# A weight's low half two steps behind its high half, and a fresh order at four borders

## The reference, cut to what matters

```python
def swiglu(x, w_gate, w_up, w_down):                 # D_MODEL = 1024, D_FF = 2816
    return (jax.nn.silu(x @ w_gate) * (x @ w_up)) @ w_down

# block 1:  x + 0.5 * swiglu(rms_norm(x)), mixer, x + 0.5 * swiglu(rms_norm(x))
# block 2, per layer l, for the sequence h and (not after the last mixer) the context hc:
mod = jax.nn.silu(c) @ w_ada[l] + b_ada[l]           # nine vectors: shift, scale, gate, three times
h = h + HALF * gt1 * swiglu_2(ada_norm(h, g_ffn1[l], sh1, sc1), w1_ffn1[l], w3_ffn1[l], w2_ffn1[l])
# then a mixer of three branches, then a second feed-forward network, and at the end a norm
```

## Time and profile before

| what | value |
|---|---|
| time, median of 3 runs | 2787.03 us (2784.63 to 2797.26) |
| time of the profiled execution | 2783.03 us |
| its span, first to last instruction | 2781.2 us |
| PE busy | 2639.6 us, 95% of the span |
| DVE busy | 1713.1 us, 62% |
| ACT busy | 1060.0 us, 38% |
| TensorE's granted clock, mean | 0.970 |
| from HBM | 377.40 MB, 136 GB/s over the span |

### The profile page before, as it was taken

The page is one execution under the profiler, slowest core; times in us unless marked ns, Lnnn a source line. Parts: engine busy times, 40 slices in busy tenths (PEclk is TensorE's granted clock), DMA queues, the critical chain, the costliest instruction groups (busy, mean ns, idle before and its releaser), DMA issues.

```text
span 2781.2 us, 38461 instructions
## 1 busy us (share of the span) xinstructions
PE 2639.6 (95%) x15690; PEld 2305.1 (83%) x15690; DVE 1713.1 (62%) x2717; ACT 1060.0 (38%) x1594; POOL 142.0 (5%) x112
## 2 busy tenths in 40 slices
PE   7999878899999999998999999999999999989998
PEld 7997778899888888766878888888888887689898
DVE  6767464677767656655645567756545446766664
ACT  5445432445422223333243422323322224454553
POOL 0001023000000000032010000000000000310000
PEclk9999889899999999999999999999999999999999
DMA  7774200477455543211323255543444433135564
GB/s 246 231 231 163 71 22 1 132 247 229 143 182 172 183 152 113 58 38 46 99 86 104 84 192 179 170 157 121 138 141 130 134 106 112 57 122 179 168 190 151
DMA packets 110113, 380.97 MB, mean 137 GB/s; under 512 B 12017, under 2 KB 17393, under 8 KB 109553
## 3 DMA queue, kind: packets, MB, share of 16 engines
q1 hardware_dynamic: 108928, 373.32, 42.1%
q10 hardware_dynamic: 1008, 5.18, 0.5%
HBM read 377.40 MB, written 1.05 MB: 136 GB/s over the span
## 4 chain that ended last, share of the span: by engine, by line
PE 86%; DVE 7%; ACT 4%; issue 2%; POOL 1%; DMA 1%; SPq 0%; ACTq 0%; DVEq 0%
PE B L1363 25%; PE B L1365 24%; PE B L1364 24%; PE B L1585 2%; DVE w_lo L1914 2%; ACT w_hi L1654 1%; POOL TMP L2338 1%; PE B L1601 1%; PE B L1378 1%; PE B L1509 1%; PE B L1379 1%; PE B L1380 1%; PE B L1495 1%; PE B L1502 1%; DVE AC L2175 1%
## 5 line engine op out<-in xcount | busy, mean ns | idle before, releaser
L1363 PE MATMUL B<-U,w_hi 128*128 128x256 f32 (+1 forms) x2896 | 959.9, 331 | 9.4 <-DVE w_lo L1914 5.6
L1364 PE MATMUL B<-U,w_hi 128*128 128x256 f32 (+1 forms) x2896 | 953.4, 329 | 0.0
L1365 PE MATMUL B<-U,w_lo 128*128 128x256 f32 (+1 forms) x2896 | 953.0, 329 | 0.0
L1914 DVE TENSOR_TENSOR w_lo<-w_raw,w_hi 128x1024 fp32r<-128x1024 f32 (+4 forms) x587 | 685.2, 1178 | 414.0 <-ACT w_hi L1654 413.3
L1654 ACT ACTIVATE w_hi<-w_raw 128x1024 fp32r<-128x1024 f32 (+4 forms) x587 | 591.0, 1012 | 519.0 <-PE B L1365 487.1
L1363 PEld LDWEIGHTS B<-U,w_hi 128*128 128x128 f32 x2896 | 549.0, 190 | 67.7 <-issue 13.2
L1364 PEld LDWEIGHTS B<-U,w_hi 128*128 128x128 f32 x2896 | 549.2, 190 | 52.5 <-issue 1.3
L1365 PEld LDWEIGHTS B<-U,w_lo 128*128 128x128 f32 x2896 | 548.6, 189 | 51.7
L1363 PE MATMUL B<-HHf,w_hi 128*128 128x256 f32 (+1 forms) x1122 | 363.9, 324 | 5.8 <-DVE w_lo L1914 5.8
L1364 PE MATMUL B<-HLf,w_hi 128*128 128x256 f32 (+1 forms) x1122 | 362.8, 323 | 0.0
L1365 PE MATMUL B<-HHf,w_lo 128*128 128x256 f32 (+1 forms) x1122 | 362.8, 323 | 0.0
(11 more groups left out here) (337 smaller groups left out, 2675.5 us busy)
## 6 DMA issues: line engine op xcount, KB each, us to landing
w_raw<-in_w SPq DMA_DIRECT2D x504, 512.0 KB, 4.3
w_ada<-in_w SPq DMA_DIRECT2D x144, 512.0 KB, 3.5
w_raw<-in_w SPq DMA_DIRECT2D x58, 384.0 KB, 3.5
w_raw<-in_w SPq DMA_DIRECT2D x16, 240.0 KB, 2.6
X<-in_x SPq DMA_DIRECT2D x2, 1024.0 KB, 9.6
w_raw<-in_w SPq DMA_DIRECT2D x8, 256.0 KB, 3.1
BW<-in_bias ACTq DMA_DIRECT2D x1, 1536.0 KB, 10.4
K<-in_consts ACTq DMA_DIRECT2D x2, 640.0 KB, 4.5
```

Source lines behind the costliest of these rows:

```text
L1363: pe.matmul(o, hi, xh, start=i == 0 and s.start, stop=False)
L1364: pe.matmul(o, hi, xl, start=False, stop=False)
L1365: e = pe.matmul(o, lo, xh, start=False, stop=i == last and s.stop)
L1914: dve.tensor_tensor(w_lo[:, plan.slot[u], 0:n], w_raw[:, plan.ring[u], 0:n], w_hi[:, plan.slot[u], 0:n].bitcast(F32), ALU.subtract).then_i ...
```

## The change

It has five parts. The split of a unit becomes two steps: `split_hi` stands where `split` stood, and `split_lo` follows when LATER = 2 more steps have been put down, or at once if the next step uses the unit. SP's refill of `w_raw` goes with the low half. At the borders the generator advances by 2, 0, 3 and 1 tiles at its four places instead of 3, 0, 3 and 3, and the two tiles that are left come behind the context's `x_add`. In f10, f20 and f11 the modulation is spread over 27 turns instead of 28. Ahead of both output projections of block 2 stands an `exp_table`. No arithmetic changes.

```diff
--- before.py
+++ after.py
@@ -17,7 +17,7 @@
 NF = FF // 128
 EPS = 1e-6
 UC = 1024
-NR, NH, AHEAD = 4, 3, 2
+NR, NH, AHEAD, LATER = 4, 3, 2, 2
 SC = 96 ** -0.5
 
 
@@ -25,7 +25,7 @@
 
 ADA = {"f1": 12, "f2": 12, "f10": 48, "f20": 48, "f11": 24, "f21": 0}
 
-ADAS = {"f1": 28, "f2": 25, "f10": 28, "f20": 28, "f11": 28, "f21": 28}
+ADAS = {"f1": 28, "f2": 25, "f10": 27, "f20": 27, "f11": 27, "f21": 28}
 
 COLS1 = [("ffn1_norm", 8), ("mix_norm", 8), ("ffn2_norm", 8), ("final_norm", 8), ("conv_w", 60),
          ("gdn_norm_w", 1), ("q_norm_w", 1), ("k_norm_w", 1), ("dt_bias", 8), ("a_log", 8)]
@@ -218,7 +218,7 @@
 
         cut = [u for u in range(len(self.units)) if not self.raw_only(u)]
         place = {u: i for i, u in enumerate(cut)}
-        steps, used, done, top = [], set(), 0, 0
+        steps, used, done, top, late = [], set(), 0, 0, []
         self.slot = {u: i % NH for u, i in place.items()}
         self.ring = {u: i % NR for u, i in place.items()}
         self.cut = cut
@@ -236,11 +236,17 @@
                 at = place[u] if u in place else place[top] + 1
                 top = max(top, u) if s.kind != "ahead" else top
                 while done < min(at + AHEAD + 1, len(cut)) and (done < NH or cut[done - NH] in used):
-                    steps.append(Step("split", u=cut[done]))
+                    steps.append(Step("split_hi", u=cut[done]))
+                    late.append([LATER, cut[done]])
                     done += 1
+
+            while late and (not late[0][0] or late[0][1] in turns and s.kind not in ("fetch", "ahead")):
+                steps.append(Step("split_lo", u=late.pop(0)[1]))
             if s.kind not in ("fetch", "ahead"):
                 steps.append(s)
                 used |= {wt[0] for wt in s.wts if wt[3]}
+                for x in late:
+                    x[0] -= x[0] > 0
         self.steps = steps
 
 
@@ -306,9 +312,8 @@
                 if not work:
                     rb = stat.rsqrt_half(0, D)
                     work = self.ada_half(*norm, 0, rb)
-                if turn != 1:
-                    for _ in range(3):
-                        next(work, None)
+                for _ in range((2, 0, 3, 1)[turn]):
+                    next(work)
                 turn += 1
             self.x_add((*name, m, 1), 256, b, gate, 256)
             stat.half(1, "X", m, ("x_add", (*name, m, 1)))
@@ -999,6 +1004,7 @@
             yield from branch(0, "CV", "wpw", 3, conv, alone)
 
         beside(main(), taps())
+        self.add("exp_table")
         stat = Stat(self, f"wout{l}", n)
         for m in range(8 if l else 5):
             b = self.gemm((f"wout{l}", m), [(f"wout{l}", k, 128 * m, 128) for k in range(8)], n, x=f"Y{l}",
@@ -1646,7 +1652,7 @@
                 w.each(s.need)
                 act.dma_start(M2[s.key]["K2"][:], consts2[:, 0:640]).then_inc(*landed(f"k2{s.key}", 0))
                 act.dma_start(M2[s.key]["K3"][:], consts2[:, 640:1920]).then_inc(*landed(f"k3{s.key}", 0))
-            elif k == "split":
+            elif k == "split_hi":
                 u, n = s.u, plan.units[s.u][1]
                 w.wait_ge(*at(f"w{plan.ring[u]}", u))
                 if plan.over[u] is not None:
@@ -1908,7 +1914,7 @@
                                          MOD[:, l, b, 0:1]).then_inc(*up("ada_x", s.key))
                 dve.tensor_tensor_reduce(raw, raw, CS[:, 1, :], 1.0, 0.0, ALU.mult, ALU.add,
                                          MOD[:, l, b, 1:2]).then_inc(*up("ada", s.key, ("unit", u)))
-            elif k == "split":
+            elif k == "split_lo":
                 u, n = s.u, plan.units[s.u][1]
                 w.wait_ge(*at("w_hi", u))
                 dve.tensor_tensor(w_lo[:, plan.slot[u], 0:n], w_raw[:, plan.ring[u], 0:n],
@@ -2359,7 +2365,7 @@
             sp.dma_start(w_ada[:, i, :], source(u)).then_inc(*landed(f"a{i}", u))
         more, rows = plan.cut[NR:], plan.rows[2:]
         for s in plan.steps:
-            if s.kind == "split" and more:
+            if s.kind == "split_lo" and more:
                 u = more.pop(0)
                 w.wait_ge(*at("w_lo", s.u))
                 sp.dma_start(w_raw[:, plan.ring[u], 0:plan.units[u][1]], source(u)).then_inc(*landed(f"w{plan.ring[u]}", u))
```

## The result

The changed kernel takes 2911.0 us (median of 4 runs, 2909.7 to 2912.5) against 2785.8 (4 runs of the kernel before on the same chip): ratio 1.0443, 95% interval 1.0411 to 1.0475, about 125 us slower. The profiled execution took 2911.7 us, with a span of 2909.8 and a granted clock of 0.970 as before.

The account below looks back on a forecast made before the run. PE, busy 95% of the span, was taken as the bound. From 2783.0 us, 103.2 lost less 21.5 won gave 2864.7; 18.7 for clock falls made 2883, range 2838 to 2918 (high end: every addition at its worst).

Parts of the forecast that it names:

- Down tiles: At tile ends PE waits for addition plus low half: 22 long stalls of 2.29 us, 23 short of 1.83; 7 off.
- The clock: In the new stalls: the clock falls at half of the long ones, 11 x 1.7 = 18.7 us; short ones free.
- The gate and up tiles: At n = 256, 0.72 us lost in each of 19 turns with modulation, 13.7 us; other turns and n = 512 nothing.
- Borders: Behind f10, wout0, f20 and f11, the context's addition comes earlier: 3 us each, 12 us won.
- clock behind them: After the four border waits, half of the time at the lower clock comes back: 8.2 us won.
- table: Behind wout1, `exp_table` takes a table load out of the path: 1.28 us, counted as 1.3 won.
- smaller places: Behind f1 `sq_add` comes later, 2 us; in the first mixer a low half behind a copy, 2 us: 4 lost.
- Refills: SP's refills, moved with the low halves, land 4.3 us after issue against 5.4 available: hidden, by 1.1 us.
- Clock holds: Rival: no new stall lowers the clock, 2865 us; chance 0.30.
- falls at all: Rival: the clock falls at every stall, short ones too, 2941 us; chance 0.08.
- Covered: Rival: DVE reaches low halves sooner, so down tiles cost nothing; 2772 us, no change that can be told; chance 0.05.
- faster: Rival: PE's waits for low halves go entirely and the borders win their 21.5, 2747 us; chance 0.04.

Follow-up runs that it names:

- e3: Changed kernel with low halves still to come put ahead of every x_add: 2801.1 us, ratio 1.0055 to the kernel before.
- e1: Changed kernel with LATER = 0, each low half right behind its high half, other edits kept: 2772.0 us, ratio 0.9953 to the kernel before.
- e9: Kernel before with border order and 27 turns, without parted split and early table load: 2771.8 us, ratio 0.9935.
- e10: Changed kernel with low halves still to come put ahead of each network's first product only: 2897.3 us, ratio 1.0401 to the kernel before.
- e4: Changed kernel with low halves still to come put ahead of every gate and up product: 2869.9 us, ratio 1.0311 to the kernel before.
- e5: Kernel before with the border order (2, 0, 3, 1) alone: 2771.6 us, ratio 0.9930.

## Why the prediction was right, and where its sum was off

The forecast was 2883 us, in a range of 2838 to 2918; it came to 2911, near the upper end. The sign and the mechanism were right; 28 us are missing, most of them in one term. (The terms that I named for the high end add up to 2923, not 2918; the result lies under both.)

**Down tiles.** Forecast 50.4 + 42.1 - 7 and 18.7 for the clock, 104 us; e3 got 108 back. The places and the count were right, each with an addition and a low half between, but for wout1's end, whose wait of 2.38 us is 2.49 in e3 and 2.38 in e1. The size was a little low: a long end costs 2.47 us in place of 2.29, a short one 2.0 (tiles of 9.47 for 7.48) in place of 1.83. I took 0.06 us from the end of a low half to PE's start, from a place where the wait was short; here DVE ends at about 1046.24 + 1.22 = 1047.46 and PE starts at 1047.60, and its first matmul takes 0.30 instead of 0.23.

**The clock.** I put a fall at half of the long stalls, 11 x 1.7 = 18.7. It came at 4 of 22 long ones, and at 2 short ones in f21, where I had left it out: 6 x 1.64 = 10 (19.07 - 17.43 = 1.64). So the forecast erred to the high side here and the stalls to the low side by about as much; that the two cancel is luck. Two more falls came behind first turns, where I had not looked; they count below. The stretches around one fall:

```profile
1042.00:1049.10 7.10, 4.91 (x23) 3.75 (x22) 3.66 (x5) 1.85 (x3) 0.00 (x0) 1.00 0.08 16
1049.10:1052.50 3.40, 3.40 (x10) 2.63 (x9) 2.65 (x5) 0.00 (x0) 0.00 (x0) 0.50 0.78 269
```

The clock goes to 0.50, the lower level of 1.2 GHz, 1.5 us after PE has started again, behind an idle time of 2.19 us; in f21 it does so behind 1.80 us. By the rule cited in the forecast (the Trainium skill, TensorE: Matmul & The Clock Gate, section Why this matters for your kernels) no stall of this length lowers the clock. The trace does not agree; most stalls of the same length, though, stay at full clock, and no run here says what decides. The length alone does not: of the waits of 2.69, 2.78 and 2.67 us in the first turns of f1, f2 and f21, the longest has no fall behind it.

**The gate and up tiles.** This is the term that failed: 13.7 us for turns with modulation, 0 for a turn without, 0.1 in each of 63 turns only in the range. They cost 37. The step was that a low half ending at 69.39 and due at 69.43 loses nothing. f21, which has no modulation, DVE and PE:

```profile
2759.82 0.42 DVE L1960 TENSOR_TENSOR TMP<-TMP,B 128x256 f32<-128x256 f32 x1 [2.18 <-PE B L1371]
2760.73 0.43 DVE L1962 TENSOR_TENSOR HLf<-TMP,HHf 128x256 fp32r<-128x256 f32 x1 [0.49 <-ACT HHf L1718]
2761.07 2.35 DVE L1920 TENSOR_TENSOR w_lo<-w_raw,w_hi 128x1024 fp32r<-128x1024 f32 x2
2765.61 0.42 DVE L1960 TENSOR_TENSOR TMP<-TMP,B 128x256 f32<-128x256 f32 x1 [2.18 <-PE B L1371]
```

```profile
2762.26 0.28 PE L1371 MATMUL B<-U,w_lo 128*128 128x256 f32 x1
2762.43 0.36 PE L1369 MATMUL B<-U,w_hi 128*128 128x256 f32 x1
2762.63 0.28 PE L1370 MATMUL B<-U,w_hi 128*128 128x256 f32 x1
2762.75 0.28 PE L1371 MATMUL B<-U,w_lo 128*128 128x256 f32 x1
```

The product waits for PE, and the two low halves behind it start 1.25 us after it. The first ends at about 2762.29; PE starts at 2762.43 and its next steps are 0.17 and 0.20 us where 0.12 is the rule. No idle time stands in the row, since a matmul's record outlasts its step, so the list of waits does not show it. The turn takes 2765.61 - 2759.82 = 5.79 us for 5.44. The late start is not all of it: this turn ran at the slower of the two paces of the last section, at which a turn of f21 without a late half takes 5.65 us (e9). At the faster pace, in f21 of e10, the late start alone makes 5.70, by steps of 0.28 and 0.19 us where 0.11 is the rule:

```profile
2743.33 0.28 PE L1371 MATMUL B<-U,w_lo 128*128 128x256 f32 x1
2743.61 0.36 PE L1369 MATMUL B<-U,w_hi 128*128 128x256 f32 x1
2743.80 0.28 PE L1370 MATMUL B<-U,w_hi 128*128 128x256 f32 x1
2743.92 0.28 PE L1371 MATMUL B<-U,w_lo 128*128 128x256 f32 x1
```

Sixty such turns, with more in those with modulation, make 24 to 26 us. How much of that is the pace stays open; with the order put back, in e4, all of it is gone.

The other 11 to 13 are the first turns, which I had not looked at. At the start of f21, ACT, DVE and PE:

```profile
2699.14 1.28 ACT L1715 ACT_TABLE_LOAD   x1
2700.43 0.39 ACT L1715 ACTIVATE TMP<-B 128x256 f32<-128x256 f32 x1
```

```profile
2700.85 0.42 DVE L1960 TENSOR_TENSOR TMP<-TMP,B 128x256 f32<-128x256 f32 x1 [5.34 <-ACT TMP L1715]
...
2702.09 2.35 DVE L1920 TENSOR_TENSOR w_lo<-w_raw,w_hi 128x1024 fp32r<-128x1024 f32 x2
```

```profile
2703.46 0.36 PE L1369 MATMUL B<-U,w_hi 128*128 128x256 f32 x1 [2.67 <-DVE w_lo L1920]
```

The first product waits for silu, silu for a table load, and the low halves behind the product for both: DVE is idle for 5.34 us with work behind the waiting instruction that it could have done. In f1 and f21 the clock falls behind this wait (see e10).

**Borders, clock behind them, table, smaller places.** Forecast 12 + 8.2 + 1.3 won and 4 lost, 17.5 net. The borders' waits fell by 12.9 us, of which the order alone gives 9.8 (e5); the clock behind them stayed up (in e5 it fell behind wout0's), and half of the 20.5 us less at the lower clock in e5 is 10. Behind f1 the border's sum waits 3.21 us for 1.19, the 2 us that I gave. The early table load wins nothing that shows. Net, e1 has 13 and e5 20 us. Refills hid as forecast: behind the additions of the networks no first low half waits for its high half.

**The rivals.** *Clock holds* (2865) and *falls at all* (2941) both fell: 4 of 22 long. *Covered* (2772) and *faster* (2747) asked for stalls under 0.8 us; they are 2.47 and 2.0.

## What to carry to other kernels

On an engine that takes its work in order, look at what stands directly ahead of each operation that a busier engine will want: if that is a wait for the busier engine, the two engines take turns, and each turn costs the sum of what stands between, with a little more for the start. A cover that comes out as zero, "nothing lost, nothing left", is a loss: price it in every repetition, and look at the first repetition by itself. A profile's waits leave out losses shorter than the overlap of two records; the period from one repetition to the next shows them.

## What the runs showed of the hardware that I had not expected

Matmuls of 256 columns ran at one of two paces at full granted clock, in f21 of e9 for the whole network. Stretches of f2 (kernel before, then e1) and of f21 (e5, then e9), all without a wait of PE (us; PE, PEld, DVE, ACT, POOL busy with counts; granted clock; DMA share; GB/s):

```profile
620.00:640.00 20.00, 20.00 (x179) 20.00 (x178) 15.46 (x24) 10.78 (x16) 0.00 (x0) 1.00 0.77 248
```

```profile
620.00:640.00 20.00, 20.00 (x172) 20.00 (x171) 15.75 (x23) 9.62 (x15) 0.00 (x0) 1.00 0.69 224
```

```profile
2650.00:2670.00 20.00, 20.00 (x179) 20.00 (x178) 11.96 (x15) 9.92 (x16) 0.00 (x0) 1.00 0.60 202
```

```profile
2650.00:2670.00 20.00, 20.00 (x172) 20.00 (x172) 11.79 (x14) 9.71 (x15) 0.00 (x0) 1.00 0.55 178
```

172 matmuls in place of 179 in 20 us, 4% fewer; down tiles of 7.77 us in place of 7.48. It cost e1 5.5 us in f2 and e9 6.7 in f21 (turns 115.9 for 111.5, down tiles 62.1 for 59.8). The f21 turns of e5 and e9 hold the same instructions in the same order, so the order does not decide it; what does stays open, and with it some microseconds of every single profile here. Where PE stands still in between, the pace can change: with the stalls of e4, seven down tiles of f1 running take 9.48 or 9.75 us each, 2.0 more than at the one pace or the other.
